# A hybrid S5 / DeltaNet decoder layer: the output projection as two 64-row halves of the array

## The reference

```python
h = rms_norm(x, g_mix);  proj = h @ w_in            # 2048 -> u | qkv | z | beta | a | gates
y_s5 = ...S5 state space scan, GELU, half-GLU...    # 1024 wide
y_dn = ...gated DeltaNet, 8 heads x 128...          # 1024 wide
mix = sigmoid(gate_a) * (y_s5 @ w_a) + sigmoid(gate_b) * (y_dn @ w_b)
x = x + mix @ w_out                                 # the output projection: 2048 x 2048
h2 = rms_norm(x, g_ffn)
x = x + (silu(h2 @ w_gate) * (h2 @ w_up)) @ w_down  # 5632 wide
h3 = rms_norm(x, g_ple)
x = x + (p @ w_ple) * sigmoid(h3 @ w_ple_gate)
y = rms_norm(x, g_final)
```

## Time and profile before

| | us |
|---|---|
| median of 3 runs | 1994.21 (1993.83 to 1995.47) |
| profiled execution | 1993.93 |
| its span | 1992.2 |
| TensorE matmul busy | 1975.6 (99%) |
| VectorE busy | 1127.6 (57%) |
| ScalarE busy | 813.3 (41%) |
| out projection, first matmul to the feed-forward's first | 806.40 to 919.33 |

### The profile page before, as it was taken

One profiled execution on the slowest core, in us unless ns is written; L12 is line 12 of the kernel. 1 busy time (PEld: TensorE's weight loads), 2 busy tenths in 40 slices (PEclk: granted clock), 3 DMA queues, 4 the chain that ended last, 5 costly groups with the idle time before them and its releaser, 6 DMA issues.

```text
span 1992.2 us, 38789 instructions
## 1 busy us (share of the span) xinstructions
PE 1975.6 (99%) x15613; PEld 1936.8 (97%) x15613; DVE 1127.6 (57%) x1409; ACT 813.3 (41%) x1068; POOL 303.5 (15%) x382
## 2 busy tenths in 40 slices
PE   9999999999999999999999999999999999999998
PEld 8999999899999889999999999999999999999997
DVE  7799997873645677544444444434444444444554
ACT  7343336733434553344333333333333333334543
POOL 4956443000002110011000000000000000001111
PEclk9999999999999999999999999999999999999999
DMA  9544445544437586644544444444444444444442
GB/s 229 180 138 129 132 133 155 162 124 140 120 112 210 163 279 223 221 150 139 158 148 147 148 149 150 151 149 157 148 147 148 149 151 148 148 142 158 143 148 101
DMA packets 300837, 310.16 MB, mean 156 GB/s; under 512 B 25013, under 2 KB 290886, under 8 KB 300466
## 3 DMA queue, kind: packets, MB, share of 16 engines
q1 hardware_dynamic: 296800, 296.76, 48.4%
q0 software_dynamic: 3504, 11.64, 2.0%
q10 hardware_dynamic: 418, 0.12, 0.0%
HBM read 291.34 MB, written 17.14 MB: 155 GB/s over the span
## 4 chain that ended last, share of the span: by engine, by line
PE 93%; DVE 4%; DMA 1%; ACT 1%; issue 1%; ACTq 0%; SPq 0%; DVEq 0%
PE pg L2157 86%; DVE cacc L1742 2%; DVE wlo L1404 1%; PE side_a L2199 1%; PE side_a L2190 1%; DMA raw<-in_w_out 1%; PE side_a L2502 0%; ACT whi L957 0%; PE side_a L2157 0%; DMA par2n<-in_conv_w 0%; PE side_a L2521 0%; PE side_b L2157 0%; PE side_b L2190 0%; PE side_a L2421 0%; PE side_b L2421 0%
## 5 line engine op out<-in xcount | busy, mean ns | idle before, releaser
L1404 DVE TENSOR_TENSOR wlo<-raw,whi 128x1024 fp32r<-128x1024 f32 (+1 forms) x528 | 650.6, 1239 | 642.5 <-ACT whi L957 640.9
L957 ACT ACTIVATE whi<-raw 128x1024 fp32r<-128x1024 f32 (+1 forms) x528 | 545.1, 1039 | 907.0 <-PE pg L2157 839.9
L2157 PE MATMUL pg<-xhi,whi 128*128 128x320 f32 x2816 | 478.3, 312 | 1.4 <-ACT whi L957 1.4
L2157 PE MATMUL pg<-xhi,wlo 128*128 128x320 f32 x2816 | 470.7, 309 | 1.2 <-DVE wlo L1404 1.2
L2157 PE MATMUL pg<-xlo,whi 128*128 128x320 f32 x2816 | 470.3, 309 | 1.1 <-DVE xlo L1411 1.1
L2157 PEld LDWEIGHTS pg<-xhi,whi 128*128 128x128 f32 x2816 | 424.4, 188 | 10.6 <-issue 6.8
L2157 PEld LDWEIGHTS pg<-xhi,wlo 128*128 128x128 f32 x2816 | 427.4, 188 | 2.4 <-DVE wlo L1404 2.2
L2157 PEld LDWEIGHTS pg<-xlo,whi 128*128 128x128 f32 x2816 | 427.4, 188 | 1.4 <-DVE xlo L1411 1.4
L927 POOL TENSOR_TENSOR fsi<-fsg,inv 128x640 f32<-128x640 f32 x22 | 43.3, 1969 | 706.6 <-ACT fsg L1287 706.6
L2157 PE MATMUL pg<-mhi,wlo 128*128 128x320 f32 x704 | 118.9, 309 | 0.0
L2157 PE MATMUL pg<-mhi,whi 128*128 128x320 f32 x704 | 118.8, 309 | 0.0
(11 more groups left out here) (488 smaller groups left out, 1698.2 us busy)
## 6 DMA issues: line engine op xcount, KB each, us to landing
raw<-in_w_in SPq DMA_DIRECT2D x144, 512.0 KB, 4.1
raw<-in_w_gate SPq DMA_DIRECT2D x88, 512.0 KB, 3.5
raw<-in_w_up SPq DMA_DIRECT2D x88, 512.0 KB, 3.5
raw<-in_w_down SPq DMA_DIRECT2D x80, 512.0 KB, 3.5
raw<-in_w_out SPq DMA_DIRECT2D x32, 512.0 KB, 3.5
raw<-in_w_ple_gate SPq DMA_DIRECT2D x32, 512.0 KB, 3.5
raw<-in_w_a SPq DMA_DIRECT2D x16, 512.0 KB, 5.2
raw<-in_w_b SPq DMA_DIRECT2D x16, 512.0 KB, 4.3
```

The source lines that it names most:

```text
L957: act.activation(whi[:, r, 0:nk, :], raw[:, r, 0:nk, :], ACT.Copy).then_inc(w_hi, 1)
L1404: dve.tensor_tensor(wlo[:, r, 0:nk, :], raw[:, r, 0:nk, :], whi[:, r, 0:nk, :].bitcast(F32), ALU.subtract).then_inc(w_lo, 1)
L2157: ins = pe.matmul(out[:, m, 0:N], w[:, r, k, m * P:(m + 1) * P], a[:, k0 + k, :], start=first and k == 0 and part == 0, stop=last and k == ...
```

## The change

Each matmul of the out projection is replaced by two with 64 rows each: rows 0 to 63 of the weight tile and of the activations into one PSUM buffer, rows 64 to 127 into another. Even pairs use `side_a` and `side_b`; odd pairs use both halves of `pg`. VectorE adds first the one buffer to the residual and then, after waiting for its own first addition, the other. Two waits are added to TensorE: before the out projection, that the `on` keys have been drained from the side buffers; and before the feed-forward's first pair, that the last pair of the out projection has been added, since that pair lies in both halves of `pg`.

```diff
+        out_halves = [(side_ps["a"], side_ps["b"]), (pg[:, 0], pg[:, 1])]
...
+            def add_halves(n, b, j):
+
+                xs = xt[:, bass.ds(j * 2, 2), :]
+                upper, lower = out_halves[b]
+                dve.tensor_tensor(xs, xs, upper[:, :, 0:N], ALU.add).then_inc(sem("upper_added"), 1)
+                dve.wait_ge(sem("upper_added"), n)
+                dve.tensor_tensor(xs, xs, lower[:, :, 0:N], ALU.add).then_inc(evacuated, 1)
...
-            add_x(OUT_P, 0, 0)
+            add_halves(1, 0, 0)
...
-                    add_x(None, 1 - b, it * 2 + (1 + b))
+                    add_halves(it * 2 + (2 + b), 1 - b, it * 2 + (1 + b))
...
-                    add_x(None, 1, 7)
+                    add_halves(8, 1, 7)
...
-                            ins = pe.matmul(out[:, m, 0:N], w[:, r, k, m * P:(m + 1) * P], a[:, k0 + k, :],
-                                            start=first and k == 0 and part == 0, stop=last and k == nk - 1 and part == 2)
+                            opens, closes = first and k == 0 and part == 0, last and k == nk - 1 and part == 2
+                            if halves is None:
+                                ins = pe.matmul(out[:, m, 0:N], w[:, r, k, m * P:(m + 1) * P], a[:, k0 + k, :], start=opens, stop=closes)
+                            else:
+                                for rows, sums in zip((slice(0, HB), slice(HB, P)), halves):
+                                    ins = pe.matmul(sums[:, m, 0:N], w[rows, r, k, m * P:(m + 1) * P], a[rows, k0 + k, :],
+                                                    start=opens, stop=closes)
...
-                pair(it * 8 + (OUT_U + 4 * b), it * 2 + (OUT_P + b), 4 * b, KD, mxhi, mxlo, b, ready)
-
+                pair(it * 8 + (OUT_U + 4 * b), it * 2 + (OUT_P + b), 4 * b, KD, mxhi, mxlo, b, ready, out_halves[b])
+
+            for j in range(H // 2):
+                wait_drained(pe, ("on", j))
...
+                if c == 0:
+                    pe.wait_ge(evacuated, OUT_P + 8)
                 gate_up(0, 0, ffn_in if c == 0 else None)
```

More of the change, by code:

```diff
@@ L2144, in end, with unit @@
                 ins.then_inc(filled[fill_at[key][0]], 1)
-            def unit(u, r, par, k0, nk, first, last, hi, lo, out=None, lows_ready=None):
+            def unit(u, r, par, k0, nk, first, last, hi, lo, out=None, lows_ready=None, halves=None):
                 out = pg[:, par] if out is None else out
@@ L2563, in _, with pair @@
                     unit(n, n % RING, p % 2, UK * j, nk, j == 0, j == pair_units[p] - 1, *operands[kind], lows_ready=lows_ready)
-            def pair(u0, p0, du, kts, hi, lo, par, ready=None):
+            def pair(u0, p0, du, kts, hi, lo, par, ready=None, halves=None):
                 pe.wait_ge(evacuated, p0 - 1)
@@ L2572, in pair @@
                     jj = du + j
-                    unit(u0 + j, jj % RING, par, UK * j, min(UK, kts - UK * j), j == 0, j == nu - 1, hi, lo)
+                    unit(u0 + j, jj % RING, par, UK * j, min(UK, kts - UK * j), j == 0, j == nu - 1, hi, lo, halves=halves)
             def out_pair(it, b, ready=None):
-                pair(it * 8 + (OUT_U + 4 * b), it * 2 + (OUT_P + b), 4 * b, KD, mxhi, mxlo, b, ready)
+                pair(it * 8 + (OUT_U + 4 * b), it * 2 + (OUT_P + b), 4 * b, KD, mxhi, mxlo, b, ready, out_halves[b])
+            for j in range(H // 2):
+                wait_drained(pe, ("on", j))
             out_pair(0, 0, lambda j: pe.wait_ge(sem("mix_ready"), 2 * (j + 1)))
```

## The result

The change takes 1997.6 us (median of 17 executions, 1996.09 to 1999.64) against 1994.26 for the kernel before on the same chip (17 executions, 1992.96 to 1995.47): a ratio of 1.0016, 95% interval 1.0009 to 1.0023. The forecast was 1996.8, with a range of 1987.5 to 2007.5. The ratio lies inside "within 0.2%", on the slow side; the upper end of its interval lies just past it. The profiled execution took 1997.05 us with a span of 1995.3, 3.1 more than the span of before.

The account below looks back on a forecast made before the run. TensorE, busy 99% of the span, was taken to bound the kernel. Couples +0.4, wait +2.1 and tiling +0.1 gave +2.6 us on 1993.93, so 1996.5, and 1996.8 us for the median; range 1987.5 to 2007.5.

Parts of the forecast that it names:

- Couples: Out projection on TensorE: two 64-row halves run side by side in 0.1475 us against 0.147 per matmul, +0.4 us.
- rival 1: Out projection: halves hide a weight load's 0.013 us, a couple takes 0.136, total 1988 us; chance 0.16.
- Rival 2: Out projection: two loads each disturb the streams, a couple takes 0.160 us, total 2006.5 us; chance 0.13.
- Issue of twice the instructions: Out projection on TensorE: issuing 1536 matmuls and as many loads costs nothing, with a sevenfold margin.
- Code of the loop: Out projection's loop: the doubled body costs nothing in code fetches, at worst +6.8 us.
- VectorE's second addition: Out projection: eight more additions of 0.82 us stay hidden within the stage, cost nothing.
- The wait before the feed-forward: Between out projection and feed-forward: TensorE waits for both last additions, +2.08 us, none of it recovered.
- Change of tiling: Into and out of halves around the out projection: 0.09 us each over the stream, together +0.1 us, bounds 0 and 0.2.
- Nothing later becomes late: Feed-forward after the wait: the last pair's `xlo`, about 0.9 us later, is still ready before its read; no added cost.
- The stretch: From the out projection's first matmul to the feed-forward's first: 112.9 us before, forecast about 115.4.
- The starts of a couple: Out projection, expected sign in the profile: the two halves of a couple start some 0.01 us apart.
- Rival 3: Out projection: halves take turns, bound by two loads (+58 us, 2054) or two matmuls (+113, 2109); chance 0.14.

Follow-up runs that it names:

- e3_last_pair_whole: The change, but the last pair goes back to 128 rows and one addition, without the wait before the feed-forward; 1994.75 us, ratio 1.0003.
- f1_change_third: The changed kernel without any edit, loaded and measured a third time; 1996.7 us, ratio 1.0014 to the kernel before.
- e4_same_rows: The change, but both matmuls of a couple read rows 0 to 63, with rows 64 to 127 left out; 2110.18 us in one execution.

## Why the prediction was right, and where it was short

- **Couples, +0.4 (0 to 1.5).** Right. 147.04 to 147.08 ns in every profile of halves, against 147.05 and 146.5 in profiles of before: 0 to +0.4 us. The reading behind it, that the 0.147 is the matmul's own length and no load's share, was the step on which rivals 1 and 2 turned. It stood on one interval at a change of tiling; the runs with 256 and 512 columns bear it out for all but a fixed 3.5 ns, and the halves did not hide those either. The rule of the Trainium skill, "TensorE: Matmul & The Clock Gate", Part 3, that a weight load overlaps matmuls in flight only where row groups differ, would by the prediction's reckoning have given 1988 us; the runs go against it, as the earlier trace rows did.
- **Issue of twice the instructions, 0.** Right: 1536 matmuls in the 112.81 us without an idle moment.
- **Code of the loop, 0 (up to +6.8).** Right in time. The fetches did double, and hide:

```profile
q8 instruction: 6, 0.10, 0.3%
```

   (packets, MB, share, 806 to 922 us; three and 0.05 in the earlier trace rows). No idle of TensorE goes with them.
- **VectorE's second addition, 0 within the stage.** Right: 5 us more work in a stretch where it has nearly 50 to spare, and TensorE waits for nothing in the loop.
- **The wait before the feed-forward, +2.08.** Forecast as 0.35 + 0.82 + 0.04 + 0.82 + 0.05; measured 0.34 (920.63 - 920.29), 0.82, 0.03, 0.82, 0.06, sum 2.07. But that is the whole gap, from the last couple's start to the next matmul's, and the prediction put all of it into the sum. Before, the gap was one matmul's interval, 0.14, so only +1.93 comes on top. The 0.1 of starting again behind the gap is not in the sum.
- **Change of tiling, +0.1.** Right in kind (0.23 in place of 0.147 where it is seen), too small to tell in a time: the one at the start lies behind ScalarE's split.
- **What was missing: what TensorE does after it has stood still.** The prediction ended the account of the wait with "Nothing later becomes late". No other instruction did, but TensorE itself may run at half its clock for 3.4 us, +1.5 us, in more than half of the executions (23 of 39 of the change are in the upper cluster). That is the piece between the stretch's +1.95 and the +2.1 to +3.9 of the medians, together with starts that vary by up to 2.6 us between profiles. The forecast of 1996.8 is 0.8 short, and lies inside the lower cluster.
- **How near the forecast came is in part luck.** The stretch was forecast at 115.4 and is 114.88: +0.14 from the interval counted into the wait, and the rest from the +0.4 and +0.1 of couples and tiling, which this pair of profiles doesn't show. That excess of 0.5 made up for a part of the clock's 1.5, which the sum left out.
- **The starts of a couple** were forecast 0.01 apart and are 0.02, without a price.
- **Rival 3's mechanism** exists, where the halves are on the same rows, at its forecast price. (Its cheaper form, two loads, comes to 2052 by the prediction's own terms, not 2054.) Rival 2 and rival 1 have none of their signs: the pace of the couples is 0.147, not 0.160 or 0.136.

Stretch +1.95 = gap +1.93 + couples and tiling 0 (0.4 by the other profile of before). That step is shown by taking the wait away (`e3_last_pair_whole`, 113.14), by shortening it (114.0), and by adding it alone to the kernel before (113.58).

## What to carry to other kernels

Here two half-array matmuls side by side cost what one whole matmul costs, 0.147 us, so splitting rows gains nothing where the whole array is already used; what the split does cost is what must follow it, here a second addition in front of the next stage. Price a wait from the last matmul's start to the next one's start, take off the interval that was there, and ask where another buffer would let the next stage go on. And where TensorE otherwise runs without a pause, an idle of some 2 us can cost more than its length (1.5 us more here, in more than half of the executions): look at the granted clock behind it in more than one profile, and at whether the executions fall into two groups.

## What the runs showed of the hardware that was not expected

- The granted clock fell to its lower level at a gap of 2.07 us between matmul starts (1.77 idle) in two of five profiles with an idle gap of about that length. Once (`f1_change_third`) it fell 1.4 us after the gap, for 3.4 us, and cost 1.5 us; once (`e4_same_rows`) it fell inside the gap, for 6.8 us, and what follows took 2.5 us more. In the three profiles with a gap of 1.22 (0.9 idle) it was not seen there.
- Behind a gap of 1.2 to 2.1 us, at full clock, the first eight matmuls take 1.24 to 1.28 us in place of 1.17.
- An fp32r matmul on 128 rows takes 0.448 ns a column and 3.5 ns: 118.2, 147 and 232.9 ns for 256, 320 and 512 columns. On 64 rows it takes as long. This is 53% of the 0.84 a column of a plain f32 record, of which a plain matmul leaves two.
- Two fp32r matmuls on different 64-row groups run together in 147 ns, on the same group one after the other in 293.
